# A two-block model on one core: the first expert head's scores from unnormed x, and two loads begun earlier

## The chip, the core and the metric

One core of a Trainium2 chip runs the whole program in one launch. TensorE (PE) multiplies, VectorE (DVE), ScalarE (ACT) and GpSimd (POOL) work beside it, SyncE (SP) issues most loads, POOL the indirect ones. The metric is the device time of one execution in microseconds; less is better. Everything is float32, with 256 tokens of width 1024.

## What is computed

Block 1 mixes attention and a short convolution, and adds an expert layer behind a second norm. Block 2 (two layers of gated attention) follows. The change touches the passage from the mix to the experts:

```python
x = x + gate1 * (y_mix @ w_out)
h2 = rms_norm(x, norm2_w) * (1.0 + scale2) + shift2
x = x + gate2 * peer_ffn(h2, ...)

def peer_ffn(h, ...):                 # by blocks of 128 tokens
    q = (hb @ peer_wq).reshape(B, Q_BLOCK, PEER_HEADS, 2, PEER_HALF)
    s = einsum('bqhpd,hpnd->bqhpn', q, peer_subkeys)   # 8 heads, 2 halves, 128 keys
    vals, idx = lax.top_k(s, 16)
    combo = vals[..., 0, :, None] + vals[..., 1, None, :]
    ...
    top_s, pos = lax.top_k(combo, 16)                  # 16 of 16384 experts a head
    g = softmax(top_s)
    a = gelu(einsum('bqhkd,bqd->bqhk', peer_u[expert], hb))
    return einsum('bqhk,bqhkd->bqd', g * a, peer_v[expert])
```

`mod = silu(c) @ w_ada + b_ada` gives shift, scale and gate (48 column tiles of 128).

## The kernel before

The program is written by hand, engine by engine; the order of the work is the order of the code in five functions (SP, POOL, ACT, PE, DVE), and semaphores tie them. The 256 tokens are two tiles of 128. Up to the experts, x lies turned: `xT[:, c, :]` is chunk c of 8 (128 features) by 256 tokens. `aux` and `pj` are PSUM.

*Output products.* PE computes the eight chunks of `y_mix @ w_out` (`held_out`, `whole`, L1410 to L1412); DVE adds each chunk to `xT` (L2146, the last one in two halves, L2155), with weight splits (L696) and dot products for `mod` (`ada_dots`, L1919) in between; ACT squares it (L1161 to L1167). `out_sums` (PE, L1643) adds the squares by a matrix of ones.

*Second norm.* ACT takes the root (L1170), for both tiles; `second_norm` (DVE) inverts it (L1949) and scales all 16 pieces (L1951, `hT = xT * gain * rstd`); ACT adds the shift (`shift`, L1177). `keep_busy` (L1459) gives PE four products without use meanwhile.

*First head of tile 0.* `early_scores_of_head_0`: 16 query products on PE (L1720) as the chunks get ready, copies on ACT (L1198), two products with the keys (L1726), a copy of the scores (L1200) into `s_all`. `route_in_two` (DVE) finds the 8 best picks first (L2278 to L2263), which lets POOL begin, then the other 8 (L2287 on). `last_ada_tiles` (L1930) computes the last two tiles of `mod` there, which only the end of the expert layer needs.

*The gather.* For each of 2 tiles x 8 heads (16 groups `g`) x 16 picks POOL issues one indirect load (L985): 128 rows of 8 KB, one for each token, the expert's u and v side by side. They lie in 11 or 12 places (`PLACES`, `ROUNDS`: 11 in the first round) cut from memory that the first part leaves; the first 11 wait for what lies there still (for instance `queries` 2 to 8), later ones for `pair_used` of the pick before in that place. For each pick DVE multiplies u by h2 (L2223), ACT sums the row (L1224); four at a time ACT applies gelu (L1235, with a table load) and scales diagonal matrices (L1240), and PE adds v times that diagonal (`sum_pair`, L1694), which frees the place. DVE routes two groups ahead, in quarters between the row products (L2172 to L2209).

*The other scores.* On PE stand, in order: `turn_h2(0)` (L1656), `score_query(0)` for tile 1 (L1669), `score_keys(0)` (L1682), the same for heads 1 and 2 for both tiles, then the sums of picks 0 to 3, with the queries of later heads in between. ACT copies queries (L1186) and scores (L1192) out of PSUM.

*Loads.* SP issues in the order of `LOAD_ORDER`, behind it `last_ada` (two tiles of 512 KB), and four expert weights (`HELD_QUERY` and `LAST_QUERY`, 1 MB each, `SUB_UNITS`), each to places of their own, and the first weight of block 2 (L856 to L863). Behind the gather SP loads block 2's weights.

Of the kernel before, what the change touches and what calls it, by code (L numbers as in the profile page):

```python
# [126 lines left out]
OWN_GROUPS = ((OWN_UNIT, ), (HELD_QUERY, *SUB_UNITS), FIRST_HEADS, (LAST_QUERY, N1))  # L127
EARLY_UNIT = UNITS_1.index(queries_of(2))
# [229 lines left out]
def build(nc, a, out):  # L358
    ctx = ExitStack()
    with ctx:  # L360
# [42 lines left out]
        ystat = sb("ystat", [P, NT, 2])  # L403
        top8 = sb("top8", [P, NT, 8])
# [68 lines left out]
        assert w3.at <= 4096  # L473
        count16 = sb("count16", [P, PICKS], I32)
# [95 lines left out]
        def at(l, per, k):  # L570
# [7 lines left out]
        early_added, early_query, early_query_out, early_scores, early_scores_out = (  # L578
            sem("early_added"), sem("early_query"), sem("early_query_out"), sem("early_scores"), sem("early_scores_out"))
# [235 lines left out]
        def _(sp):  # L815
# [21 lines left out]
            for n in LOAD_ORDER:  # L837
# [168 lines left out]
        def _(act):  # L1006
# [157 lines left out]
            act.wait_ge(early_added, 1)  # L1164
            nc.scalar.activation(sq[:, KC - 1, 0:P], xT[:, KC - 1, 0:P], ACT.Square).then_inc(squares, 1)
            act.wait_ge(taken_dve, KC)
            nc.scalar.activation(sq[:, KC - 1, P:T], xT[:, KC - 1, P:T], ACT.Square).then_inc(squares, 1)  # L1167
            for t, ts in enumerate(halves_):
                act.wait_ge(sums, 2 + t)
                nc.scalar.activation(rstd[:, ts], aux[:, 2 + t, 0:P], ACT.Sqrt, bias=eps[:, 0:1], scale=1.0 / D).then_inc(std_ready, 1)  # L1170
# [223 lines left out]
        def _(pe):  # L1394
# [60 lines left out]
            def keep_busy(n, b):  # L1455

                pe.wait_ge(const_ready, 13)
                for _ in range(n):
# [1170 lines left out]
```

## Time and profile before

| | |
|---|---|
| median of 3 runs | 1158.73 us (1158.66 to 1159.65) |
| span of the profiled execution | 1157.0 us |
| PE, DVE, ACT, POOL busy | 1039.9, 852.6, 704.8, 345.4 us |
| gather: bytes, share of 16 DMA engines | 268.45 MB, 56.0% |
| chain that ended last | PE 53%, DMA 29%, ACT 9%, DVE 7% |

The profile covers one execution; its time is the span beside the runs' median, and its own time outside the span isn't given. The page cuts the span in 40 slices with the busy share of each engine, the granted clock of PE and the bytes that DMA moved. A timeline lists instructions in order of time, merged where they follow each other, with the idle time ahead of them in brackets; the chain of waits follows the last instruction back to what released each step; windows give busy times in a stretch that one chooses. PE entries come in pairs, two for each float32 product.

### The profile page before, as it was taken

The page shows a single profiled execution, that of the slowest core. Times are in us where ns is not written, and L with a number is a line of the kernel's source. Part 1 is how long each engine was busy: PE and PEld are TensorE (multiplying, and loading weights), DVE is VectorE, ACT ScalarE, POOL GpSimd, SP SyncE. Part 2 cuts the span into 40 slices and gives each one's busy share as a digit, 9 for nine tenths or more (in the row PEclk, how much of TensorE's full clock was granted, in tenths as well). Part 3 has the DMA queues.
Part 4 walks back from the last instruction along what each step waited for, and adds up shares of the span by engine and source line. Part 5 has one row for each costly group of instructions (what it writes and reads, how often), then busy time and mean ns, then how long its engine had stood idle before and what let it go on. Part 6 is the DMA issues. An engine that isn't in the chain of part 4 may idle for free.

```text
span 1157.0 us, 13373 instructions
## 1 busy us (share of the span) xinstructions
PE 1039.9 (90%) x4675; PEld 721.1 (62%) x4675; DVE 852.6 (74%) x1535; ACT 704.8 (61%) x1393; POOL 345.4 (30%) x367
## 2 busy tenths in 40 slices
PE   8999999998999869788877878689999999999997
PEld 6999987454455423333333333289788888888885
DVE  7998988776667666666677676646687768886776
ACT  3635835867766766666677666662458555577451
POOL 1001005554554544545544545555000000400000
PEclk9999999999999998889998989999999999999999
DMA  9986879999999999999999999999854654455540
GB/s 372 407 330 241 348 272 395 422 421 421 422 421 421 421 421 422 419 421 412 421 422 421 421 408 423 421 421 421 360 213 167 246 182 182 169 195 184 208 154 37
DMA packets 59557, 390.00 MB, mean 337 GB/s; under 512 B 6882, under 2 KB 7906, under 8 KB 15715
## 3 DMA queue, kind: packets, MB, share of 16 engines
q0 software_dynamic: 36864, 268.45, 56.0%
q1 hardware_dynamic: 21152, 120.10, 27.3%
q8 instruction: 37, 0.61, 0.2%
q10 hardware_dynamic: 1474, 0.60, 0.2%
q14 instruction: 30, 0.24, 0.1%
HBM read 388.08 MB, written 1.05 MB: 336 GB/s over the span
## 4 chain that ended last, share of the span: by engine, by line
PE 53%; DMA 29%; ACT 9%; DVE 7%; issue 2%; SPq 0%; POOL 0%; ACTq 0%; DVEq 0%; POOLq 0%
DMA rows<-in_peer_uv,work 16%; PE aux L1694 14%; DMA low_pairs<-in_peer_uv,work 10%; PE pj L1751 6%; PE pj L1753 6%; PE pj L1752 6%; PE pj L1809 5%; PE aux L1700 3%; PE pj L1810 3%; PE pj L1410 2%; PE pj L1412 2%; PE pj L1411 2%; ACT rows L1224 2%; PE aux L1669 2%; ACT L1235 2%
## 5 line engine op out<-in xcount | busy, mean ns | idle before, releaser
L1694 PE MATMUL aux<-rows,work 128*128 128x512 f32 x504 | 250.6, 648 | 51.6 <-ACT work L1240 51.6
L1694 PEld LDWEIGHTS aux<-rows,work 128*128 128x128 f32 x504 | 101.7, 206 | 186.8 <-issue 118.0
L985 POOL DMA_INDIRECT rows<-in_peer_uv,work x146 | 140.8, 964 | 243.2 <-PE aux L1694 160.1
L1694 PE MATMUL aux<-low_pairs,work 128*128 128x512 f32 x356 | 168.1, 619 | 33.8 <-ACT work L1240 33.8
L1224 ACT ACTIVATE rows<-rows 128x1024 f32<-128x1024 f32 x134 | 141.1, 1053 | 92.0 <-DVE rows L2223 91.8
L1694 PEld LDWEIGHTS aux<-low_pairs,work 128*128 128x128 f32 x356 | 69.2, 198 | 126.9 <-issue 80.4
L765 DVE TENSOR_TENSOR wlo<-wring,whi 128x1024 fp32r<-128x1024 f32 x98 | 121.1, 1251 | 32.3 <-ACT whi L759 31.5
L1224 ACT ACTIVATE low_pairs<-low_pairs 128x1024 f32<-128x1024 f32 x97 | 102.0, 1052 | 65.4 <-DVE low_pairs L2223 65.3
L759 ACT CAST whi<-wring 128x1024 fp32r<-128x1024 f32 x98 | 101.4, 1050 | 50.7 <-PE pj L1810 26.1
L985 POOL DMA_INDIRECT low_pairs<-in_peer_uv,work x101 | 97.5, 966 | 110.2 <-PE aux L1694 92.8
L2223 DVE TENSOR_TENSOR rows<-rows,aux 128x1024 f32<-128x1024 f32 x66 | 79.9, 1219 | 52.1 <-DMA rows<-in_peer_uv,work 51.6
L2223 DVE TENSOR_TENSOR rows<-rows,pj 128x1024 f32<-128x1024 f32 x68 | 82.5, 1218 | 47.5 <-DMA rows<-in_peer_uv,work 47.0
L2223 DVE TENSOR_TENSOR low_pairs<-low_pairs,pj 128x1024 f32<-128x1024 f32 x51 | 62.1, 1219 | 41.8 <-DMA low_pairs<-in_peer_uv,work 41.2
L1809 PE MATMUL pj<-x_parts,whi 128*128 128x512 f32 x256 | 90.9, 398 | 0.1
L1240 ACT ACTIVATE work<-work 128x128 f32<-128x128 f32 x248 | 79.4, 390 | 9.4 <-POOL work L955 4.0
L2223 DVE TENSOR_TENSOR low_pairs<-low_pairs,aux 128x1024 f32<-128x1024 f32 x46 | 55.8, 1219 | 37.7 <-DMA low_pairs<-in_peer_uv,work 37.4
L1410 PE MATMUL pj<-x_parts,whi 128*128 128x256 f32 x256 | 73.4, 287 | 0.3 <-DVE wlo L696 0.2
L1751 PE MATMUL pj<-whi,x_parts 128*128 128x512 f32 x184 | 72.5, 394 | 0.0
L1411 PE MATMUL pj<-x_parts,whi 128*128 128x256 f32 x256 | 72.4, 283 | 0.0
L1412 PE MATMUL pj<-x_parts,wlo 128*128 128x256 f32 x256 | 72.4, 283 | 0.0
L1810 PE MATMUL pj<-x_parts,wlo 128*128 128x256 f32 x256 | 71.8, 280 | 0.0
L1753 PE MATMUL pj<-wlo,x_parts 128*128 128x512 f32 x184 | 71.7, 390 | 0.0
(339 smaller groups left out, 2051.0 us busy)
## 6 DMA issues: line engine op xcount, KB each, us to landing
wring<-in_w SPq DMA_DIRECT2D x74, 1024.0 KB, 4.8
rows<-in_w_ada SPq DMA_DIRECT2D x46, 512.0 KB, 9.4
rows<-in_w SPq DMA_DIRECT2D x3, 1024.0 KB, 11.5
low_pairs<-in_w SPq DMA_DIRECT2D x3, 1024.0 KB, 10.2
rows<-in_peer_uv,work POOLq DMA_INDIRECT x146
work<-in_late_rows SPq DMA_DIRECT2D x2, 1024.0 KB, 9.1
xT<-in_gate_rows SPq DMA_DIRECT2D x2, 1024.0 KB, 8.0
rows<-in_norm_rows SPq DMA_DIRECT2D x2, 1024.0 KB, 6.9
```

What stands on the lines that cost most here:

```text
L759: nc.scalar.copy(layer_part("hi", l, p), layer_raw(l, p)).then_inc(w_hi, 1)
L765: dve.tensor_tensor(layer_part("lo", l, p), layer_raw(l, p), full(layer_part("hi", l, p)), ALU.subtract).then_inc(w_lo["d"], 1)
L985: pool.indirect_dma_start(out=pair(n), out_offset=None, in_=a["peer_uv"], in_offset=bass.IndirectOffsetOnAxis(ap=expert[g % EXPERTS][:, j: ...
L1224: nc.scalar.activation(pair(n)[:, 0:D], pair(n)[:, 0:D], ACT.Copy, accum_out=dots[g % 2][:, j:j + 1]).then_inc(dotted, 1)
L1410: mm(o, w[0], x[0], start=start, stop=False, skip_group_check=skip)
L1411: mm(o, w[0], x[1], start=False, stop=False, skip_group_check=skip)
L1694: ins = mm(peer_sum[t][:, half(c)], diag[:, n % PICKS, :], pair(n)[:, D + c * 512:D + (c + 1) * 512], start=(n % (EXPERT_HEADS * PICKS) == ...
L1751: mm(bank(u), hi[:, k, ts], w_hi_[:, j, :], start=(k == 0), stop=False)
L1753: ins = mm(bank(u), hi[:, k, ts], w_lo_[:, j, :], start=False, stop=(k == last))
L1809: mm(both, w_hi_[:, k, :], x_parts[:, :, k, :], start=(k == 0), stop=False, skip_group_check=True)
L1810: ins = mm(bank(u)[:, 0:T], w_lo_[:, k, :], xh[:, k, :], start=False, stop=(k == KC - 1), skip_group_check=True)
L2223: v.tensor_tensor(row, row, h2_tok[g // EXPERT_HEADS], ALU.mult).then_inc(multiplied, 1)
```

## The change

The scores are linear in h2. For one token, with r its inverse root mean square, h2 = r * (x * gain) + shift2, so the first head's scores are r times those of `x * gain` plus those of the shift. The change computes them so for tile 0:

- ACT writes `xg = xT * gain` behind each square (`gain_x`), and the shift beside it as a 129th column.
- PE runs the 16 query products on `xg` (129 columns) between the sums of squares (`early_products`), in two portions.
- The keys are multiplied with the 128 columns (bank 0) and, spread over all tokens, with the 129th (bank 1); ACT copies the latter to `s_all`, DVE adds the former times r by token (`scores_of_head_0`). r by token is the diagonal of `rstd` (`rstd_by_token`).
- The norm of tile 0 is cut in two halves around `route_first`, tile 1 and `route_rest` follow; ACT's `root(1)` and all shifts stand behind the score copy.
- `keep_busy` goes. `turn_h2(0)` waits for all of the shift of tile 0.
- The last two tiles of `mod` are computed among the output chunks, and `last_ada` and `HELD_QUERY` are loaded behind the queries of head 4, as soon as the mixed input is split.

```diff
+                if n == MIXED_DONE:
+                    sp.wait_ge(mix_split, HC + NT)
+                    sp.dma_start(last_ada, a["w_ada"][RING_TILES:].rearrange("n p d -> p n d")).then_inc(last_ada_loaded, 16)
+                    load_unit(HELD_QUERY)
             sp.wait_ge(proj, M1)
-            sp.dma_start(last_ada, a["w_ada"][RING_TILES:].rearrange("n p d -> p n d")).then_inc(last_ada_loaded, 16)
-            load_unit(HELD_QUERY)
             load_unit(LAST_QUERY)
...
+            def gain_x(c):
+
+                nc.scalar.activation(xg[:, c, 0:P], xT[:, c, 0:P], ACT.Copy, scale=gain[:, c:c + 1]).then_inc(xg_ready, 1)
...
+                if c == 0:
+                    nc.scalar.copy(xg[:, :, P:P + 1], mod[:, 3 * KC:4 * KC].unsqueeze(2)).then_inc(xg_ready, 1)
+                if c < KC - 2:
+                    gain_x(c)
...
-            shift(0)
+            root(0)
             for s in range(2):
                 act.wait_ge(early_query, s + 1)
-                nc.scalar.copy(pq[:, 0, s, 0:P], aux[:, 4 + s, 0:P]).then_inc(early_query_out, 1)
+                nc.scalar.copy(pq[:, 0, s, 0:P + 1], aux[:, 4 + s, 0:P + 1]).then_inc(early_query_out, 1)
             act.wait_ge(early_scores, 1)
-            nc.scalar.copy(s_all[:, 0, :], aux[:, 0, 0:2 * KEYS]).then_inc(early_scores_out, 1)
+            nc.scalar.copy(s_all[:, 0, :], aux[:, 1, 0:2 * KEYS]).then_inc(early_query_out, 1)
+            root(1)
+            shift(0)
             shift(1)
...
             out_sums(4, 5)
-            out_sums(6, 7)
...
+            def early_products(s, chunks):
+
+                for k in chunks:
+                    pe.wait_ge(xg_ready, k + 2)
+                    ins = mm(aux[:, 4 + s, 0:P + 1], query_of_head_0[:, k, s * P:(s + 1) * P], xg[:, k, :], start=(k == 0), stop=(k == KC - 1))
+                return ins
+
+            for s in range(2):
+                early_products(s, range(HC))
+            out_sums(6, 7, tiles=(0, ))
+            for s in range(2):
+                early_products(s, range(HC, KC)).then_inc(early_query, 1)
+            out_sums(6, 7, tiles=(1, ))
...
+                    of_shift = mm(aux[:, 1, s * KEYS:(s + 1) * KEYS], pq[:, 0, s, P:P + 1].broadcast_to([P, P]), k, start=True, stop=True)
+                    ins = mm(aux[:, 0, s * KEYS:(s + 1) * KEYS], pq[:, 0, s, 0:P], k, start=True, stop=True)
...
-            keep_busy(4, 1)
             early_scores_of_head_0()
-            pe.wait_ge(taken_dve, KC)
+            pe.wait_ge(taken_dve, KC + 1)
+            pe.wait_ge(h_ready, 2 * KC)
             turn_h2(0)
...
+            last_ada_tile(1)
+            last_ada_bias()
+            dve.wait_ge(taken_dve, KC + 1)
+            rstd_by_token()
+            second_rstd(0)
+            second_norm(0, range(HC))
+            scores_of_head_0()
...
-            route_in_two()
-            last_ada_tiles()
+            route_first()
+            second_norm(0, range(HC, KC))
+            second_rstd(1)
+            second_norm(1, range(KC))
+            route_rest()
             invert_gate(0)
```

The order of instructions at two places, by the program's own listing (counts are of products here; a line number is that of the kernel named). PE from the last sums of squares to the queries of tile 1, before:

```order
L1643 MATMUL aux<-low_pairs,ones 128x128 x8
L1459 MATMUL aux<-wsT,ident 128x256 x4
L1720 MATMUL aux<-hT,rows 128x128 x16
L1726 MATMUL aux<-rows,pq 128x128 x2
L1656 MATMUL pj<-ident,hT 128x128 x8
L1669 MATMUL aux<-hT,rows 128x128 x16
L1682 MATMUL aux<-rows,pq 128x128 x2
```

and with the change:

```order
L1658 MATMUL aux<-low_pairs,ones 128x128 x4
L1673 MATMUL aux<-work,rows 128x129 x8
L1658 MATMUL aux<-low_pairs,ones 128x128 x2
L1673 MATMUL aux<-work,rows 128x129 x8
L1658 MATMUL aux<-low_pairs,ones 128x128 x2
L1749 MATMUL aux<-rows,pq 128x128
L1750 MATMUL aux<-rows,pq 128x128
L1749 MATMUL aux<-rows,pq 128x128
L1750 MATMUL aux<-rows,pq 128x128
L1686 MATMUL pj<-ident,hT 128x128 x8
L1699 MATMUL aux<-hT,rows 128x128 x16
L1712 MATMUL aux<-rows,pq 128x128 x2
```

The query products have moved ahead of the last sums, the filler (L1459) is gone, and between the key products and the turns stands nothing.

DVE from the last chunk of x to the first routing, before:

```order
L2146 SCALAR_TENSOR_TENSOR xT<-pj,mod,xT 128x256
L2155 SCALAR_TENSOR_TENSOR xT<-pj,mod,xT 128x128 x2
L1949 RECIPROCAL rstd<-rstd 128x128
L1951 SCALAR_TENSOR_TENSOR hT<-xT,gain,rstd 128x128 x8
L1949 RECIPROCAL rstd<-rstd 128x128
L1951 SCALAR_TENSOR_TENSOR hT<-xT,gain,rstd 128x128 x8
L2278 MAX work<-work 128x8 x2
```

and with the change:

```order
L2189 SCALAR_TENSOR_TENSOR xT<-pj,mod,xT 128x256
L2200 SCALAR_TENSOR_TENSOR xT<-pj,mod,xT 128x128 x2
L1955 ISA work,mod<-work,rows 128x1024
L1955 ISA mod 128x1
L1961 TENSOR_TENSOR mod<-mod,cols 128x8
L1986 ISA work,rtok<-rstd,ident 128x128
L1986 ISA rtok 128x1
L1987 RECIPROCAL rtok<-rtok 128x1
L1975 RECIPROCAL rstd<-rstd 128x128
L1981 SCALAR_TENSOR_TENSOR hT<-xT,gain,rstd 128x128 x4
L1994 SCALAR_TENSOR_TENSOR work<-aux,rtok,work 128x256
```

Then DVE behind the first eight picks (L2263 before, L2312 with the change), before:

```order
L2261 TENSOR_TENSOR work<-work 128x128
L2262 TENSOR_REDUCE work<-work 128x2x8
L2263 SCALAR_TENSOR_TENSOR work<-work 128x8
L2287 MATCH_REPLACE work<-work 128x128 x2
L2290 MAX work<-work 128x8 x2
L2293 MAX_INDEX work<-work 128x8 x2
```

and with the change:

```order
L2310 TENSOR_TENSOR work<-work 128x128
L2311 TENSOR_REDUCE work<-work 128x2x8
L2312 SCALAR_TENSOR_TENSOR work<-work 128x8
L1981 SCALAR_TENSOR_TENSOR hT<-xT,gain,rstd 128x128 x4
L1975 RECIPROCAL rstd<-rstd 128x128
L1981 SCALAR_TENSOR_TENSOR hT<-xT,gain,rstd 128x128 x8
L2340 MATCH_REPLACE work<-work 128x128 x2
L2343 MAX work<-work 128x8 x2
```

The norm has gone from ahead of the routing to both sides of it, three quarters of it behind, and the second half of the routing comes after the norm.

## Rows read from the trace of the kernel before

**Rows 1.** Page, part 2, 40 slices of 28.9 us: what DMA moved.

```profile
GB/s 372 407 330 241 348 272 395 422 421 421 422 421 421 421 421 422 419 421 412 421 422 421 421 408 423 421 421 421 360 213 167 246 182 182 169 195 184 208 154 37
```

**Rows 2.** Windows: us, busy us (instructions) of PE, PEld, DVE, ACT, POOL, PEclk, DMA share, GB/s.

```profile
140.00:158.00 18.00, 18.00 (x154) 18.00 (x153) 16.16 (x29) 6.36 (x10) 0.00 (x0) 1.00 0.67 243
160.00:172.50 12.50, 9.94 (x72) 8.98 (x73) 9.66 (x40) 6.57 (x23) 0.16 (x1) 1.00 0.98 394
172.50:174.00 1.50, 1.50 (x16) 1.50 (x15) 1.47 (x10) 0.27 (x1) 1.20 (x2) 1.00 0.11 34
174.00:195.61 21.61, 19.75 (x99) 16.10 (x99) 17.96 (x54) 13.21 (x26) 11.46 (x13) 1.00 0.99 396
195.61:208.20 12.59, 10.58 (x34) 5.99 (x33) 12.38 (x34) 9.15 (x19) 4.88 (x5) 1.00 1.01 419
208.20:218.52 10.32, 10.32 (x34) 6.08 (x33) 8.55 (x13) 6.79 (x16) 4.90 (x5) 1.00 1.01 422
```

**Rows 3.** Chain of waits, 160 to 173 us: start, us, engine, tile, line.

```profile
161.37 0.96 DVE rstd L1949
...
167.87 0.50 PE aux L1726 x2
...
168.39 0.38 ACT work L1200
...
168.80 0.48 DVE work L2278 x2
...
172.34 1.18 POOL rows L985
```

**Rows 4.** Timeline of SP's queue: start, us, line, operation, out<-in, count.

```profile
140.59 1.47 SPq L823 DMA_DIRECT2D rows<-in_w_ada  x2
...
147.89 0.33 SPq L823 DMA_DIRECT2D rows<-in_w_ada  x1
```

**Rows 5.** Timeline of DVE, in brackets the idle time before a row.

```profile
138.72 0.69 DVE L2117 TENSOR_TENSOR x_parts<-work,x_parts 128x512 fp32r<-128x512 f32 x1 [0.44 <-ACT x_parts L1143]
...
155.81 1.22 DVE L1919 CUSTOM_DVE_ANT_0 rows<-rows 128x1024 f32<-128x1024 f32 x1
...
158.91 0.48 DVE L2146 SCALAR_TENSOR_TENSOR xT<-pj,mod,xT 128x256 f32<-128x256 f32 x1 [1.87 <-PE pj L1412]
...
165.44 2.19 DVE L1951 SCALAR_TENSOR_TENSOR hT<-xT,gain,rstd 128x128 f32<-128x128 f32 x8
...
195.62 0.48 DVE L2172 MAX8 work<-work 128x8 f32<-128x128 f32 x2
...
198.08 2.35 DVE L2223 TENSOR_TENSOR low_pairs<-low_pairs,pj 128x1024 f32<-128x1024 f32 x2
```

**Rows 6.** Timeline of PE (two entries for each f32 product).

```profile
158.71 2.35 PE L1643 MATMUL aux<-low_pairs,ones 128*128 128x128 f32 x16
...
168.19 1.04 PE L1656 MATMUL pj<-ident,hT 128*128 128x128 f32 x8
...
171.16 3.84 PE L1669 MATMUL aux<-hT,rows 128*128 128x128 f32 x32 [1.93 <-ACT hT L1177]
```

**Rows 7.** Timeline of ACT.

```profile
168.66 2.44 ACT L1177 ACTIVATE hT<-hT,mod 128x128 f32<-128x128 f32 x8
...
193.65 0.59 ACT L1192 COPY work<-aux 128x512 f32<-128x512 f32 x1 [1.26 <-PE aux L1682]
```

**Rows 8.** Windows around an idle stretch of PE, columns as in rows 2.

```profile
268.50:272.00 3.50, 0.00 (x0) 0.00 (x0) 3.46 (x18) 2.91 (x5) 1.99 (x2) 1.00 1.01 419
272.20:275.60 3.40, 3.40 (x4) 1.38 (x5) 1.99 (x3) 2.88 (x7) 0.00 (x0) 0.52 1.00 417
```

**Rows 9.** Timeline of POOL: issues of gather transfers 11, 15 and 19.

```profile
195.61 0.94 POOL L985 DMA_INDIRECT rows<-in_peer_uv,work  x1 [2.60 <-PE aux L1694]
...
208.20 0.95 POOL L985 DMA_INDIRECT low_pairs<-in_peer_uv,work  x1 [6.50 <-PE aux L1694]
...
218.52 0.95 POOL L985 DMA_INDIRECT rows<-in_peer_uv,work  x1 [4.23 <-PE aux L1694]
```

More of the change, by code:

```diff
@@ L403, in build @@
         ystat = sb("ystat", [P, NT, 2])
+        rtok = sb("rtok", [P, 1])
         top8 = sb("top8", [P, NT, 8])
@@ L473, in build @@
         assert w3.at <= 4096
+        XG_AT = 4096 + EXPERT_HEADS * 2 * KEYS
+        xg = work[:, XG_AT:XG_AT + KC * (P + 1)].rearrange("p (c n) -> p c n", n=P + 1)
         count16 = sb("count16", [P, PICKS], I32)
@@ L1453, in token_major @@
                             ins.then_inc(proj, 1)
-            def keep_busy(n, b):
-                pe.wait_ge(const_ready, 13)
-                for _ in range(n):
-                    mm(aux[:, b, 0:2 * P], ident[:, :], wsT[:, 0:2, :].rearrange("p g t -> p (g t)"), start=True, stop=True)
             pe.wait_ge(const_ready, 3)
@@ L1636, in _, with out_sums @@
                 ins.then_inc(proj, 1)
-            def out_sums(*columns):
+            def out_sums(*columns, tiles=range(NT)):
                 for k in columns:
-                    for t in range(NT):
+                    for t in tiles:
                         pe.wait_ge(squares, k + 1 if k < KC - 1 else KC + t)
@@ L1924, in ada_bias, with last_ada_tile, last_ada_bias @@
                 chain.link(v.tensor_tensor(mod[:, lo:hi], mod[:, lo:hi], cols[:, B_ADA + lo:B_ADA + hi], ALU.add))
-            def last_ada_tiles():
+            def last_ada_tile(c):
                 dve.wait_ge(last_ada_loaded, 16)
-                for c in range(LAST_TILES):
-                    tile = last_ada[:, c, :]
-                    v.tensor_tensor_reduce(tile, tile, cbc, 1.0, 0.0, ALU.mult, ALU.add,
-                                           mod[:, RING_TILES + c:RING_TILES + c + 1]).then_inc(last_ada_used, 1)
+                tile = last_ada[:, c, :]
+                v.tensor_tensor_reduce(tile, tile, cbc, 1.0, 0.0, ALU.mult, ALU.add,
+                                       mod[:, RING_TILES + c:RING_TILES + c + 1]).then_inc(last_ada_used, 1)
+            def last_ada_bias():
                 dve.wait_ge(ada_used, RING_TILES)
@@ L1942, in second_gain, with second_rstd, second_norm, rstd_by_token @@
                 chain.link(v.tensor_tensor(gain[:, :], gain[:, :], cols[:, N2W:N2W + KC], ALU.mult))
-            def second_norm():
-                for t in range(NT):
-                    ts = slice(t * P, (t + 1) * P)
-                    dve.wait_ge(std_ready, 2 + t)
-                    chain.link(v.reciprocal(rstd[:, ts], rstd[:, ts]))
-                    for c in range(KC):
-                        v.scalar_tensor_tensor(hT[:, c, ts], xT[:, c, ts], gain[:, c:c + 1], rstd[:, ts], ALU.mult, ALU.mult).then_inc(h_scaled, 1)
+            def second_rstd(t):
+                ts = slice(t * P, (t + 1) * P)
+                dve.wait_ge(std_ready, 2 + t)
+                chain.link(v.reciprocal(rstd[:, ts], rstd[:, ts]))
+            def second_norm(t, chunks):
+                ts = slice(t * P, (t + 1) * P)
+                for c in chunks:
+                    v.scalar_tensor_tensor(hT[:, c, ts], xT[:, c, ts], gain[:, c:c + 1], rstd[:, ts], ALU.mult, ALU.mult).then_inc(h_scaled, 1)
+            def rstd_by_token():
+                dve.wait_ge(std_ready, 2)
+                chain.link(v.tensor_tensor_reduce(s_left[:, 0, :], rstd[:, 0:P], ident[:, :], 1.0, 0.0, ALU.mult, ALU.add, rtok[:, :]))
+                chain.mark(v.reciprocal(rtok[:, :], rtok[:, :]))
+            def scores_of_head_0():
+                dve.wait_ge(early_query_out, 3)
+                dve.wait_ge(early_scores, 2)
+                chain.wait()
+                v.scalar_tensor_tensor(s_all[:, 0, :], aux[:, 0, 0:2 * KEYS], rtok[:, :], s_all[:, 0, :], ALU.mult, ALU.add).then_inc(early_scores_out, 1)
             for z, x_in in zip((slice(0, HC), slice(HC, KC)), x_loaded):
@@ L2151, in _ @@
                         ada_dots(34 + 2 * c, 36 + 2 * c)
+                    if c == 5:
+                        last_ada_tile(0)
                 else:
@@ L2270, in combine, with route_first @@
                 return z
-            def route_in_two():
-                first, rest = slice(0, FIRST_ROUTED), slice(FIRST_ROUTED, PICKS)
-                lists = [s_all[:, 0, s * KEYS:(s + 1) * KEYS] for s in range(2)]
+            first, rest = slice(0, FIRST_ROUTED), slice(FIRST_ROUTED, PICKS)
+            lists = [s_all[:, 0, s * KEYS:(s + 1) * KEYS] for s in range(2)]
+            def route_first():
                 dve.wait_ge(early_scores_out, 1)
```

39 lines of the change are left out of this document (18 added, 21 removed).

## The prediction

> **What bounds the kernel now.** I read the slices of the page first: the last line of its second part shows some 421 GB/s from about 175 to 810 us [rows 1]. That stretch is the gather of expert rows: 256 transfers of 128 rows by 8 KB, 1.05 MB each, issued by POOL. The windows say the same where it begins: a DMA share of 0.99 to 1.01 and up to 422 GB/s from 174 us on [rows 2]. So the gather is bound by its bytes, 1.05 MB / 421 GB/s = 2.49 us a transfer, and the rest of the program starts when it ends. What this change can win or lose is therefore a shift of that stream: when it starts, and whether its queue runs dry.
>
> Then I read the chain of waits ahead of the stream [rows 3]: the last output chunk on DVE (158.91), sums, root, reciprocal (161.37), norm and shift, the query and key products of the first head on PE, the copy of its scores on ACT (168.39), routing on DVE (168.80), the first gather at 172.34. The windows show what DMA does meanwhile [rows 2]: 394 GB/s from 160 to 172.5 us (the loads begun at 158.9), 34 GB/s until 174.0, then the gather. From 140 to 158 us it moves only 243 GB/s.
>
> **The moved loads.** Two loads of 1.05 MB each go from 158.9 us to behind the fifth head's queries, about 142 us. SP gets there at 142.06 (140.59 + 1.47 [rows 4]), and the wait put ahead of them, for the mixed input's split, ends with DVE's row at 138.72 + 0.69 [rows 5]: SP stalls for nothing, and the loads queued behind lose no time of issue. The room there is 18 us x (421 - 243) GB/s = 3.2 MB, so 2.1 MB fit. What lies behind them in the queue can land later: the last bias tile, issued at 147.89 [rows 4], has 1.6 MB of its own and its predecessor's to wait for (3.7 us) and at worst all of the 2.1 MB (5.0), 156.6, where DVE reads it at 155.81 [rows 5]; at best it is there by 153. I take 0, and keep the worst as a rival. Behind 158.9 remain 2.9 MB, 6.9 us instead of 11.8: DMA is free by about 168. Without this part the earlier gather would still have queued until 172.5. Price 0, cover: that room.
>
> **The first gather.** On PE a product of 128 columns in f32 is two entries of 0.12 us (3.84 us for 32 [rows 6]); 129 columns I take as the same, at most twice that. From the end of the output products at 158.71 [rows 6] PE now has: sums of chunks 4 and 5, 8 entries, 0.97; eight new products 1.94; sums of the last two chunks for tile 0, 0.48 (162.1, root and reciprocals leave the path); eight new products 1.94; sums of tile 1, 0.48 (164.5); then shift and key products, the third of which ACT can take 0.5 after its start, as it took the last key product (167.87 to 168.39 [rows 3]): 165.5. ACT copies 0.41 (168.39 to 168.80 before [rows 3]), DVE's new multiply-add of 256 columns from PSUM is about 0.49, as the one at 158.91 [rows 5]. Routing begins at 166.45 instead of 168.80, and the first gather at **170.0 instead of 172.34, 2.3 us earlier**.
> Beside that path: eight scalings on ACT at about 0.3 each and one tiny copy, where ACT is busy 6.4 of 18 us [rows 2]: 0. The two dot products of the last loaded tiles (1.2 each, as the one at 155.81 [rows 5]) leave DVE's way behind routing; one goes in ahead of chunk 6, into DVE's idle 1.87 us [rows 5], one behind chunk 7 while PE multiplies: 0 to 0.2. The token-wise root (a 128-column reduction and a reciprocal) and the first four norms lie before the scores arrive: 0.
>
> **What is late next.** On DVE the other four norms of tile 0 and all of tile 1 now stand behind the routing, and on ACT all shifts behind the score copy. DVE is free of the routing at 169.75; four norms 1.1 (2.19 for eight [rows 5]), reciprocal 0.96 [rows 3], then eight norms with ACT's shifts behind them, 0.4 + 2.44 [rows 7]: tile 1 is ready at 174.7. PE's next work waits for just that: the queries of tile 1 began at 171.16 [rows 6]. **They begin 3.6 us later**, and behind them stand in order 16 products (3.84), the queries of heads 1 and 2, their keys, and the first sums that free gather places.
>
> And PE has stood idle: its filler of four products is gone, so from 165.6 until the turns at 171.3 nothing runs, 5.7 us. The windows show what 3.5 us of that does [rows 8]: after an empty 268.5 to 272.0 the granted clock is 0.52, the 1.2 GHz level, for 272.2 to 275.6. The turns (1.04 us [rows 6]) run in the same shade and take some of it away. I take 1.0 us on the 3.84 of the first head's queries; bounds 0 (clock back in time) and 1.9 (all of it at the low level).
>
> Now the price of lateness. A gather place is free when PE has summed the row that lay in it, so POOL's issue of transfers 11, 15 and 19 (counted from 0) at 195.61, 208.20 and 218.52 [rows 9] follows PE and not DMA. How full the queue is then comes from the windows [rows 2]:
> - at 195.61: 21.61 us x 396 GB/s = 8.56 MB = 8.16 of 11 transfers: 2.84 left, 7.1 us;
> - at 208.20: 5.28 MB more, 13.19 of 15: 1.81 left, 4.5 us;
> - at 218.52: 4.36 MB more, 17.35 of 19: 1.65 left, 4.1 us.
>
> A transfer needs some reserve before it, or DMA idles. From the start of the stream: 1.7 us from issue (172.34) to the first bytes (174.0), and in the 21.61 us behind it 1.3 us lost (8.56 MB would take 20.3). So the reserve needed lies between 1.7 and 3.0 us; I take the middle, 2.35. The spare is then 4.7, 2.15 and 1.75 us.
> How late are these three issues? Transfer 11 waits for the first sum on PE: 3.6 + 1.0. Transfers 15 and 19 wait for the sums of rows 4 to 8, and these for the second group of row products on DVE (198.08 [rows 5]). In front of that group DVE routes head 2, which began at 195.62 [rows 5] when DVE was free. It needs ACT's copy of head 2's scores (193.65 [rows 7], 0.59 long), which is 3.6 later at 197.25 and done at 197.85: routing 2.25 late, plus the 1.0 of the clock, **3.25 us late**.
> The stream can be ahead of its old place by at most the least of: 2.3 (start), 4.7 - 4.6 = +0.1, 2.15 - 3.25 = -1.1, 1.75 - 3.25 = **-1.5**. The lead is used up at transfer 11 and turns into 1.5 us behind at transfer 19. Later the reserve grows again and the row products wait for DMA themselves, so the compute side's lateness goes, the stream's shift stays. All behind the gather moves with it.
>
> Sum: span 1157.0 + 1.5 = 1158.5 us. The profiled span lies 1.7 under the median of the runs, 1158.73, which I take as constant around it: **1160.2 us**. A measurement tells about 0.2%, 2.3 us; so I forecast no change that it can tell, on the slow side.
>
> **Rivals.**
> 1. *The lead is kept.* The reserve suffices: at the low need of 1.7, without a clock fall, the least is 2.4 - 2.25 = +0.2, and if head 2's score copy were not late as well, the full 2.3 remains. For: DMA shows 419 and 422 GB/s around the two thinnest points, no loss at 4.1 us [rows 2]; the two dot products gone from DVE (2.4 us) quicken it. Against: the order of DVE and ACT, which leaves tile 1 until last. Time: 1158.7 - 2.3 = 1156.4, with half the lead 1157.6.
> 2. *The clock of PE decides* (the slower side). At the low level through all of the first head's queries, 1.9 us, the second group is 4.2 late; at a need of 3.0 the least is 4.1 - 3.0 - 4.2 = -3.0: 1161.8. It decides once the loss passes about 1 us. For: the idle stretch is longer than the one that cost PE its clock [rows 8]; before, PE was idle 1.93 us at most there [rows 6]. Against: the turns may bring the clock back. The Trainium skill (TensorE: Matmul & The Clock Gate, Why this matters for your kernels) advises against idle gaps between bursts of products, since the clock falls back to half; by that rule the taking out of the filler is a fault of the change, and the row at 272.2 agrees. It would put the sum here, by that rule alone, at this rival's 1161.8 rather than the 1159.2 without any fall.
> 3. *The moved loads come late.* At the worst worked out above the last bias tile holds chunk 6 and all behind it by 0.8: 1161.0. For: one queue, one order; against: the 3.2 MB of room.
> 4. *The change does not do what it says*: 129 columns cost double. Then 3.9 us more lie ahead of the routing, the first gather comes at 173.9, later than before, and PE behind it as much: about 1164.
>
> **How the numbers follow.** Forecast 0.51, lead kept 0.17, clock 0.22, loads 0.05, dear columns 0.05. The forecast's own range takes the need from 1.7 to 3.0 and the clock from 0 to 1.9 us: 1158.5 to 1161.8. With part of the lead-kept case (three quarters of the lead) the lower end is 1157.0, and a little past the clock case 1162.4. Faster by over 0.2% (under 1156.4): half of rival 1 and little else, 0.1. Slower (over 1161.05): most of rival 2, rival 4, half of 3 and the forecast's tail, 0.27. Within: 0.63.
>
> **What would show it.** First gather near 170.0; DMA quiet from 168 to 171.7; PE's queries of tile 1 at 174.7 and, if the clock fell, longer than 3.84 with a granted clock under 1; transfer 11 near 200; DMA below 400 GB/s in some stretch between 195 and 222 us. Wrong, if DMA holds 420 there while the first gather is early (then it ends early), or if the first gather itself is not early.

## The result and the profile after

| | before | with the change |
|---|---|---|
| median | 1159.35 us (1158.49 to 1160.16, 21 runs) | 1161.01 us (1159.56 to 1162.67, 21 runs) |
| ratio, 95% interval | | 1.0014 [1.0008, 1.002] |
| span of the profiled execution | 1157.0 us | 1159.2 us |
| first gather issued | 172.34 us | 169.55 us |

The change makes the kernel 1.7 us slower; the forecast was 1160.2 us, 1.5 us over the median it started from. The first gather begins 2.8 us earlier and the stream that follows it still ends later.

The slices of the page look as before [rows 1]; 421 GB/s in most of the gather's slices. The loss is in one place, the seventh and eighth slice (174 to 231 us): 395 and 422 GB/s before, 381 and 372 now.

```profile
GB/s 371 406 333 237 347 295 381 372 423 422 421 422 421 421 422 421 421 422 421 421 419 421 421 413 421 422 420 420 368 207 170 250 181 181 166 198 185 202 158 37
```

The chain of waits up to the first gather, with the change. It answers to [rows 3].

```profile
164.83 0.24 PE aux L1749 x2
...
165.09 0.38 ACT work L1219
...
165.49 0.50 DVE work L1994
...
166.01 0.48 DVE work L2328 x2
```

Routing starts at 166.01 instead of 168.80, 2.8 us earlier. That is the whole gain, and POOL's timeline shows it in the first of these rows (after, transfers 0, 7, 11, 15 and 19; [rows 9] has the last three before):

```profile
169.55 1.28 POOL L991 DMA_INDIRECT rows<-in_peer_uv,work  x1 [53.56 <-DVE work L2312]
...
188.29 1.01 POOL L991 DMA_INDIRECT rows<-in_peer_uv,work  x1 [3.21 <-PE aux L1699]
...
200.23 0.94 POOL L991 DMA_INDIRECT rows<-in_peer_uv,work  x1 [2.00 <-PE aux L1724]
...
211.48 0.94 POOL L991 DMA_INDIRECT low_pairs<-in_peer_uv,work  x1 [5.16 <-PE aux L1724]
...
221.80 0.94 POOL L991 DMA_INDIRECT rows<-in_peer_uv,work  x1 [4.23 <-PE aux L1724]
```

The last three came at 195.61, 208.20 and 218.52 before: they are 4.6, 3.3 and 3.3 us late, and transfer 7, which waits for a query product (L1699), 4.8 us. Its row before:

```profile
183.47 1.01 POOL L985 DMA_INDIRECT rows<-in_peer_uv,work  x1 [0.21 <-PE aux L1669]
```

What DMA does then stands in the windows of after (columns as in [rows 2]):

```profile
169.55:171.00 1.45, 0.03 (x1) 0.06 (x1) 1.45 (x4) 1.28 (x4) 1.28 (x1) 0.50 0.00 0
...
174.00:188.29 14.29, 13.47 (x68) 12.14 (x68) 9.26 (x25) 4.29 (x11) 4.91 (x7) 0.85 1.00 419
188.29:200.23 11.94, 11.16 (x54) 8.86 (x55) 8.99 (x42) 9.16 (x19) 4.26 (x4) 1.00 0.93 338
200.23:211.48 11.25, 10.59 (x34) 6.00 (x33) 11.04 (x24) 9.08 (x19) 4.87 (x5) 1.00 0.99 400
211.48:221.80 10.32, 10.32 (x34) 6.09 (x33) 9.43 (x14) 6.78 (x16) 4.90 (x5) 1.00 0.92 340
...
221.80:229.80 8.00, 8.00 (x26) 4.13 (x25) 3.25 (x3) 6.23 (x15) 6.76 (x8) 1.00 0.98 356
```

Against 421 GB/s the stretch from 188 to 200 us loses 11.94 x (1 - 338/421) = 2.4 us, the next 0.6, then 2.0 and 1.2: 6.1 us in all. So 2.8 us ahead becomes some 3 us behind. I counted the gather's own packets as well: against the kernel before, the first transfer is delivered 2.7 us earlier, the 13th 0.1 us earlier, the 21st 3.1 us later.

Why the issues are late is on PE. Its timeline after answers to [rows 6], the windows below it to [rows 8]:

```profile
164.89 0.39 PE L1750 MATMUL aux<-rows,pq 128*128 128x128 f32 x2
170.97 1.94 PE L1686 MATMUL pj<-ident,hT 128*128 128x128 f32 x8 [5.70 <-ACT hT L1196]
174.09 5.88 PE L1699 MATMUL aux<-hT,rows 128*128 128x128 f32 x32 [1.18 <-ACT hT L1196]
```

```profile
165.30:168.30 3.00, 0.00 (x0) 0.00 (x0) 2.64 (x15) 1.58 (x6) 0.00 (x0) 0.98 0.88 309
168.30:171.00 2.70, 0.03 (x1) 0.06 (x1) 2.60 (x9) 1.28 (x4) 1.28 (x1) 0.50 0.02 9
...
174.10:178.00 3.90, 3.90 (x18) 3.90 (x19) 3.69 (x18) 0.09 (x1) 2.50 (x3) 0.50 0.99 412
178.00:179.00 1.00, 1.00 (x9) 1.00 (x9) 0.77 (x3) 0.17 (x1) 0.00 (x0) 0.80 1.04 418
179.00:182.00 3.00, 2.55 (x18) 2.28 (x17) 0.00 (x0) 1.11 (x3) 0.94 (x1) 1.00 0.99 418
```

The first of these rows is the last key product, the second the turns (`turn_h2`, eight entries), the third the queries of tile 1. PE is idle 5.7 us, its granted clock falls to 0.50, the 1.2 GHz level, and stays there until 178 us, although PE works without a pause from 174. The queries of tile 1 begin 2.9 us later than before and last 2.04 us longer. ACT and DVE hand it on, in the timelines of after that answer to [rows 7] and [rows 5]:

```profile
198.28 0.58 ACT L1211 COPY work<-aux 128x512 f32<-128x512 f32 x1 [1.26 <-PE aux L1712]
```

```profile
157.19 1.23 DVE L1945 CUSTOM_DVE_ANT_0 rows<-rows 128x1024 f32<-128x1024 f32 x1 [0.56 <-DMA rows<-in_w_ada]
...
183.25 0.16 DVE L2286 RECIPROCAL work<-work 128x1 f32<-128x1 f32 x1 [4.41 <-ACT work L1227]
...
198.89 0.49 DVE L2221 MAX8 work<-work 128x8 f32<-128x128 f32 x2 [0.55 <-ACT work L1211]
...
201.37 2.35 DVE L2272 TENSOR_TENSOR low_pairs<-low_pairs,pj 128x1024 f32<-128x1024 f32 x2
```

The copy of head 2's scores is 4.6 us late and DVE's second group of row products 3.3 us (198.08 before). DVE's first group is late by as much (183.33, 179.98 before): it waits 4.41 us for ACT, which copies the late queries first.

### The profile page after: what moved, and what is told of

Its sections match the earlier page's. It is cut to its first block, busy times and chain, and to the rows that moved or that the text cites. A ratio compares the mean times of both kernels' runs of the same rounds, so it can differ in the third digit from the quotient of the medians.

```text
span 1159.2 us, 13379 instructions
## 1 busy us (share of the span) xinstructions
PE 1041.9 (90%) x4671; PEld 723.6 (62%) x4671; DVE 852.9 (74%) x1539; ACT 706.7 (61%) x1402; POOL 344.0 (30%) x367
## 3 DMA queue, kind: packets, MB, share of 16 engines
HBM read 388.08 MB, written 1.05 MB: 336 GB/s over the span
## 4 chain that ended last, share of the span: by engine, by line
PE 54%; DMA 27%; ACT 9%; DVE 6%; issue 2%; SPq 1%; ACTq 0%; DVEq 0%
DMA rows<-in_peer_uv,work 18%; PE aux L1724 15%; DMA low_pairs<-in_peer_uv,work 6%; PE pj L1777 6%; PE pj L1779 6%; PE pj L1778 5%; PE pj L1835 5%; PE aux L1699 4%; PE pj L1836 3%; DMA rows<-in_w_ada 2%; ACT rows L1245 2%; PE pj L1431 2%; PE pj L1432 2%; PE pj L1433 2%; ACT L1256 2%
## 5 line engine op out<-in xcount | busy, mean ns | idle before, releaser
L1724 PE MATMUL aux<-rows,work 128*128 128x512 f32 x504 | 244.9, 636 | 44.2 <-ACT work L1261 44.2
L1724 PE MATMUL aux<-low_pairs,work 128*128 128x512 f32 x356 | 174.4, 639 | 39.2 <-ACT work L1261 39.2
```

Of the source, the lines that this page charges most:

```text
L1724: ins = mm(peer_sum[t][:, half(c)], diag[:, n % PICKS, :], pair(n)[:, D + c * 512:D + (c + 1) * 512], start=(n % (EXPERT_HEADS * PICKS) == ...
```

## The experiments

Two theories stood first. **T1**: PE, DVE and ACT are late, so the issues of transfers 7 to 19 are, the queue runs dry and the early start is lost. **R1**: the moved loads cost the time, with the last bias tile that lands late (the first DVE row above, 0.56 us). A ratio is to the kernel before, run beside it, with its 95% interval; what is read of the stream comes from one profiled execution of each kernel, which can lie up to 1.6 us off the median (the loads back: 1159.84 against 1161.41). One transfer is 1.05 MB, 2.49 us at 421 GB/s.

### Filler where PE idled

```diff
             early_scores_of_head_0()
+            keep_busy(12, 4)
...
             turn_h2(0)
+            keep_busy(3, 4)
             pe.wait_ge(h_ready, 3 * KC)
```

Expected: 

> Changed kernel plus 12 filler products between the early scores and the turns, and 3 between the turns and the first head's queries of tile 1, in the place where PE idled 5.7 and 1.2 us. T1 (late compute work decides: the queries of tile 1, 2.9 us late at their start and 2.0 us longer at the low clock, hand the lateness to the sums and dot products that free the gather's places): the turns take 1.04 instead of 1.94 us, the queries 3.84 instead of 5.88, the second group of dot products comes about 2 us earlier (199.3 instead of 201.37), transfer 19 is issued near 219.8 instead of 221.80, and the time falls by 2 us, to about 1159.0. Rival R1 (the moved loads and the late bias tile cost the time): 1161.0, unchanged. Rival R2 (the order of the norms alone, the clock a side matter because DVE waits for other things): queries 3.84, but the second dots less than 0.7 us earlier and the time 1160.5 or more.

Measured: 1159.63 us, ratio 1.0002 [0.9993, 1.0011]. Its PE timeline (the passage begins 1.0 us later in this execution; DVE was as late at chunk 5 already, 156.01 instead of 155.02, and then waited 0.78 us for the last bias tile, where it was 0.56):

```profile
171.98 1.06 PE L1686 MATMUL pj<-ident,hT 128*128 128x128 f32 x8 [0.53 <-ACT hT L1196]
...
175.09 3.84 PE L1699 MATMUL aux<-hT,rows 128*128 128x128 f32 x32 [0.75 <-ACT hT L1196]
```

Turns and queries take what they took before. Of the loss of 1.7 us the clock is worth some 1.4 (1.0014 against 1.0002, with intervals that overlap a little), where T1 said 2.0. The second group of row products begins at 200.33, 1.0 us earlier, or 2.0 with the late passage taken off. R1 expected no change, and so is not the whole cause; R2 expected less than 0.7 us there and 1160.5 us or more, and is out.

### The loads back at their old place

```diff
-                if n == MIXED_DONE:
-                    sp.wait_ge(mix_split, HC + NT)
-                    sp.dma_start(last_ada, ...).then_inc(last_ada_loaded, 16)
-                    load_unit(HELD_QUERY)
             sp.wait_ge(proj, M1)
+            sp.dma_start(last_ada, ...).then_inc(last_ada_loaded, 16)
+            load_unit(HELD_QUERY)
...
             route_rest()
+            last_ada_tile(0)
+            last_ada_tile(1)
+            last_ada_bias()
```

Expected: 

> Changed kernel with the two loads back at their old place behind the last output chunk, and the two dot products on their tiles and the bias back behind the routing. T1 (late compute work decides at transfers 7 to 19): the stream's first bytes come later, near 172.5 to 173.5, the stream is not ahead at its start, but the issues of transfers 11 to 19 move less than 0.5 us against the changed kernel and the time stays within 0.7 us of it, about 1161.0. R1 (the moved loads and the tile that lands late cost the time): about 1159.0, 2 us faster. A third possibility, that the early start does carry through: 1.5 to 2 us slower, 1162.5 to 1163.

Measured: 1161.41 us, 1.0022 [1.0013, 1.0031]: no faster, so R1 falls. Here the second part of the change is worth nothing that can be told, since what it brings is lost behind it anyway.

### Tile 1 ahead of the rest of tile 0

With the filler (all 15 products in one place); on DVE and PE (ACT's second root and its shifts follow the same order):

```diff
             route_first()
-            second_norm(0, range(HC, KC))
             second_rstd(1)
             second_norm(1, range(KC))
+            second_norm(0, range(HC, KC))
             route_rest()
...
-            pe.wait_ge(h_ready, 2 * KC)
-            turn_h2(0)
-            pe.wait_ge(h_ready, 3 * KC)
+            pe.wait_ge(h_ready, 2 * KC + HC)
             score_query(0)
+            pe.wait_ge(h_ready, 3 * KC)
+            turn_h2(0)
```

Expected: 

> Changed kernel with filler on PE (15 products) and with tile 1's root, reciprocal, norm and shift ahead of the last four chunks of tile 0; PE does the queries of tile 1 ahead of the turns of tile 0. T1: queries of tile 1 begin at about 172.6 instead of 174.09 and take 3.84, so they end at 176.4 instead of 179.97, 3.5 us earlier; second dots near 198, transfer 19 issued near 218.3 to 219; the stream keeps most of its lead of up to 2.8 us and the time is 1157.5 (1156.6 to 1158.5). R1 (loads): 1161.0. R2 (order alone, the clock a side matter): as the run with filler alone less 1.5 us, about 1159.

Measured: 1158.32 us, 0.9993 [0.9984, 1.0002]: inside the expected range, 0.8 us over its middle. The queries began at 173.07, and issues 15 and 19 come only 0.4 us later than in the kernel before. Yet the windows show the queue thin, from issue 15 to 19 and behind 19:

```profile
208.58:218.90 10.32, 10.32 (x34) 6.09 (x33) 10.00 (x14) 6.79 (x16) 4.89 (x5) 1.00 0.97 380
218.90:226.90 8.00, 8.00 (x26) 4.12 (x25) 3.00 (x4) 6.23 (x15) 6.78 (x8) 1.00 0.94 353
```

The stream was 2.5 us ahead when 13 transfers were delivered and 0.2 when 21 were. T1 holds in kind, but a stream that starts earlier needs its later issues earlier too.

### The kernel before, with PE late

```diff
             turn_h2(0)
+            keep_busy(15, 1)
             pe.wait_ge(h_ready, 3 * KC)
             score_query(0)
```

Expected: 

> Kernel before, with 15 filler products between the turns and the first head's queries of tile 1: these then begin near 176.3 instead of 171.16 and end near 180, as in the changed kernel, while the first gather stays at 172.34 and the loads at their old place. T1: the issues of transfers 11, 15 and 19 come at about 200, 211.5 and 221.8, as in the changed kernel, and the time is the changed kernel's within 0.7 us, 1161 (what the early start brings is lost whole at the thin places). If the lead counts one for one: 2.8 us more than the changed kernel, 1163.8. If DMA's backlog hides the lateness (R1): 1159.3, as the kernel before.

Measured: 1161.11 us, 1.0021 [1.0012, 1.003], the changed kernel's time without any part of the change. Lateness on PE is enough, and when it is there the early start is worth nothing that shows. The two are not late by quite the same: issue 15 comes at 210.76 here and at 211.48 in the changed kernel, so up to 0.7 us of a gain could hide in the comparison.

### The moved loads alone

The kernel before with the loads at the mixed split and the dot products on their tiles beside chunks 6 and 7, as in the change.

Expected: 

> Kernel before with the moved loads alone: the two loads issued at the mixed split, one dot product ahead of chunk 6's end and one behind chunk 7, the bias behind them; scores of the first head as before. T1 (how late the compute work frees the places decides, and in the kernel before the row products of group 0 wait for the third and fourth gathered row, 1.2 us each): first gather 172.3 to 172.5, first bytes up to 0.5 us earlier, the 2.6 us freed on DVE at 177.2 end in the waits for those rows; issue of transfer 19 within 0.5 us of the kernel before, time within 0.6 us of it, 1159.0. R1 (moved loads and the bias tile that lands late cost time): 1160.5 to 1161. If the freed DVE time counts: 1157 to 1158.

Measured: 1159.67 us, 1.0007 [0.9998, 1.0016], no difference that can be told. The first gather stays at 172.37, DVE's freed time ends in waits for rows, and issue 19 is where it was. One thing was not expected: PE idles 1.93 us ahead of the queries, as before [rows 6], and here the clock falls.

```profile
171.19 5.47 PE L1672 MATMUL aux<-hT,rows 128*128 128x128 f32 x32 [1.93 <-ACT hT L1180]
```

```profile
172.50:175.90 3.40, 3.40 (x18) 3.40 (x17) 3.23 (x17) 0.27 (x1) 2.79 (x3) 0.50 0.46 123
```

### Tile 1's reciprocal ahead of the scores

The run with tile 1 first, changed further (the rest of tile 0's norm, its turns and ACT's shifts behind tile 1's, as there):

```diff
-            second_norm(0, range(HC))
+            second_norm(0, range(2))
+            second_rstd(1)
             scores_of_head_0()
...
-            keep_busy(15, 4)
+            keep_busy(4, 4)
+            pe.wait_ge(h_ready, KC + 2)
+            turn_h2(0, range(2))
+            keep_busy(9, 4)
```

Expected: 

> The run with tile 1 first, and in it tile 1's reciprocal ahead of the scores' multiply-add (two norms of tile 0 ahead of the scores instead of four) and two of tile 0's eight turns in PE's gap. T1: scores 0.3 us later, queries of tile 1 begin at 172.0 instead of 173.07, copy of head 2's scores near 194.1 instead of 195.37, second dots near 197.1, now set by the landing of the fourth gathered row; transfer 19 issued 0.8 to 1.3 us earlier than in the kernel before (217.2 to 217.7); time 1157.3 (1156.8 to 1158.0). If the reserve of the queue and not the issue decides: no better than the run it is made from, 1158.3.

Measured: 1157.05 us, 0.9986 [0.9977, 0.9995], faster than both kernels. The first gather is at 170.25, 2.1 us ahead of the kernel before; issues 15 and 19 come 0.1 us earlier than there, not 0.8 to 1.3: T1's time came out, its way there did not. The stream is 1.7 us ahead after 21 transfers and 2.1 at its end, with nearly full rate in the same two windows:

```profile
208.10:218.42 10.32, 10.32 (x34) 6.08 (x33) 9.54 (x14) 6.79 (x16) 4.90 (x6) 1.00 1.01 421
218.42:226.42 8.00, 8.00 (x26) 4.12 (x25) 4.20 (x4) 6.23 (x15) 6.79 (x8) 1.00 1.01 415
```

### The same with a late first gather

```diff
                     pool.wait_ge(first_routed, 1)
+                    pool.wait_ge(h_ready, 2 * KC + 2)
```

Expected: 

> The kernel of the previous run with one wait more: POOL issues the first gather only when the first two chunks of tile 0 and all of tile 1 are shifted, near 172, as late as in the kernel before. Tells what the early start itself carries once PE and DVE are early. T1 (the start counts through the landing of the fourth row, that is, for its 1 to 1.3 us and no more): transfer 19 issued as in the kernel before within 0.4 us, time 1158.3 to 1159.0. If the start does not count at all: as the previous run, 1157.3. If it counts in full: 2.3 to 2.8 us more than the previous run, 1159.6 to 1160.

Measured: 1160.39 us, 1.0012 [1.0003, 1.0021]. The wait held the first gather until 173.68, 1.3 us later than in the kernel before and 3.4 later than in the run above:

```profile
173.68 1.18 POOL L992 DMA_INDIRECT rows<-in_peer_uv,work  x1 [57.37 <-ACT hT L1197]
```

The time is 3.3 us more than that run's. So the start counts in full here, and T1's 1 to 1.3 us for it, by way of the fourth row, was wrong. The rival named in the expectation (in full) holds: its 2.3 to 2.8 us were meant for a start near 172.

### Four products of filler

```diff
             early_scores_of_head_0()
+            keep_busy(4, 4)
```

Expected: 

> Changed kernel with four filler products of 256 columns, as many as the change took out, behind the early scores: PE idles 3.8 instead of 5.7 us ahead of the turns. If the taking out of the filler alone cost the clock, it is at 1.0 here (turns 1.04, queries 3.84 us); if the longer wait for the norms does, it falls again (turns up to 1.94, queries over 4.5 us). The 3.5 us gap at 268.5 in the kernel before was followed by the low level, so the second is the likelier; time 1160 to 1161.

Measured: 1162.32 us, in a single run, over the 1160 to 1161 expected. PE idles 3.98 us, and the turns and queries:

```profile
171.11 1.71 PE L1686 MATMUL pj<-ident,hT 128*128 128x128 f32 x8 [3.98 <-ACT hT L1196]
174.23 5.72 PE L1699 MATMUL aux<-hT,rows 128*128 128x128 f32 x32 [1.41 <-ACT hT L1196]
```

In this execution the four products that the change took out do not hold the clock; the longer wait for the norms makes the gap.

### The queries chunk by chunk, from either order

What the runs so far say together is **T2**: the stream keeps its early start whole unless an issue finds the queue nearly empty. Both kernels of this test let PE begin with the first shifted chunk (in the second, 2 stands for `HC`; the filler is 12 products in the first, 4 and 7 in the second):

```diff
                     for k in range(KC):
+                        if h == 0 and s == 0:
+                            pe.wait_ge(h_ready, KC + HC + k + 1)
                         ins = mm(aux[:, 4 + s, ts], ...)
```

The first is made from the run with tile 1 first (start 2.8 us early, lead lost). Expected: 

> The run with tile 1 first (first gather 2.8 us early, which lost its lead at transfers 14 to 20), and in it PE begins the first head's queries of tile 1 with the first shifted chunk instead of the last; 12 filler products instead of 15. The runs so far give a sharper theory, T2: the stream keeps its early start whole as long as each issue from 7 to 19 finds at least about 1.2 transfers in the queue (1.27 found: no loss; 0.8 found: 2.4 us lost), and a lead can be lost but lateness saved beyond that brings nothing. T2 here: queries end near 175.2 instead of 176.9, second dots near 197, issues 15 and 19 about 1 to 1.4 us earlier than in the run it is made from, 1.2 or more transfers left there, the stream 2.5 us or more ahead to its end, time 1156.2 (1155.7 to 1156.9). If the issues alone decide, one for one: 1157.0 to 1157.3. If what was lost in the earlier run was the price of DMA's own sharing with the loads: 1158.3, as that run.

Measured: 1156.92 us, 0.9979 [0.9969, 0.9988]. The queries start at 171.05 instead of 173.07, issue 15 comes 1.2 us earlier than in the kernel before (1.6 earlier than in the parent), and of 2.8 us 2.4 are kept, where the parent kept 0.2. The time lies between the two expectations; the stream speaks for T2, since the issues one for one would leave it 0.2 + 1.6 = 1.8 us ahead. But issue 15 found 1.0 transfers, not the 1.2 expected. The windows of the two stretches:

```profile
206.99:217.31 10.32, 10.32 (x34) 6.08 (x33) 9.75 (x14) 6.78 (x16) 4.91 (x6) 1.00 1.01 414
217.31:225.31 8.00, 8.00 (x26) 4.12 (x25) 4.25 (x6) 6.23 (x15) 6.78 (x8) 1.00 1.01 396
```

The second is made from the run with the reciprocal early (lead kept). Expected: 

> The run with tile 1's reciprocal early (first gather 2.1 us early, no lead lost, 1157.05), with the same start of the queries chunk by chunk; filler 4 and 7 products. T2: issues 15 and 19 come 1 to 1.5 us earlier than in the run it is made from and nothing follows from it, since no issue there found the queue too thin: stream 1.7 to 2.1 us ahead, time within 0.5 us of that run, 1157.0. If the issues decide one for one: 1155.6 to 1156.0.

Measured: 1156.86 us, 0.9983 [0.9974, 0.9992]: issues 15 and 19 come 1.8 us earlier than in its parent and the time is the parent's within 0.2 us, where the issues one for one would have brought about 1 us or more. DMA was at full rate from issue 15 to 19 in both:

```profile
206.31:216.63 10.32, 10.32 (x34) 6.08 (x33) 9.10 (x13) 6.79 (x16) 4.89 (x5) 1.00 1.01 421
```

An issue ahead of need is worth nothing, as T2 said.

### The loads back once more, where the lead is kept

The second of these two, with the edit of the second experiment. Expected: 

> The run with tile 1's reciprocal early and the queries chunk by chunk (1156.86), with the two moved loads back at their old place and the dot products on their tiles back behind the routing: the second part of the change undone where the first one keeps its lead. T2 (the early start counts in full unless an issue finds less than about 1.1 transfers queued): the stream's first transfers 0.4 to 1.0 us later, since the loads still move when the gather starts; the 2.6 us more on DVE end for the most part in the wait for the fourth gathered row, second dots 0 to 1 us later, 1.2 to 1.6 transfers left at issue 15, so no further loss: 0.4 to 1.2 us more than the run it is made from, 1157.3 to 1158.0. If the loads' place is worth nothing: 1156.9. If DVE's 2.6 us come in whole, the queue runs thin again: 1158.5 or more.

Measured: 1158.06 us, 0.9992 [0.9983, 1.0001], 1.2 us more (1.0 by the ratios, whose intervals overlap). The first gather is issued at the same time (170.04), but the stream is 1.3 instead of 2.3 us ahead, from its first transfers on, with 418 GB/s or more from issue 11 to 8 us behind issue 19. So the moved loads are worth about 1 us, once nothing takes it away; the stream shows it more clearly than the times do.

### The runs side by side

Times against the kernel before, us (first gather, issue 15, and the time at which the gather's packets have delivered 21 transfers; minus is earlier). "Left" is worked out as in the prediction, the issue's number less GB/s x us of the windows since the gather's first bytes, in transfers.

| run | first gather | issue 15 | left at 15 | GB/s 15 to 19 | left at 19 | GB/s in 8 us behind 19 | stream at 21 |
|---|---|---|---|---|---|---|---|
| before | 0 | 0 | 1.81 | 422 | 1.65 | 421 | 0 |
| the change | -2.8 | +3.3 | 0.42 | 340 | 1.08 | 356 | +3.1 |
| filler | -1.8 | +2.3 | 0.71 | 365 | 1.11 | 366 | +2.0 |
| four products of filler | -2.7 | +3.3 | 0.46 | 356 | 0.95 | 347 | +3.0 |
| loads back | -2.7 | +3.4 | 0.32 | 356 | 0.82 | 372 | +2.4 |
| tile 1 first | -2.8 | +0.4 | 0.62 | 380 | 0.88 | 353 | -0.2 |
| before, PE late | 0 | +2.6 | 0.58 | 371 | 0.92 | 348 | +2.1 |
| loads alone | 0 | 0 | 1.58 | 421 | 1.43 | 423 | -0.6 |
| reciprocal early | -2.1 | -0.1 | 1.12 | 421 | 0.98 | 415 | -1.7 |
| late first gather | +1.3 | +3.4 | 1.08 | 415 | 0.99 | 377 | +2.5 |
| chunks, tile 1 first | -2.8 | -1.2 | 1.01 | 414 | 0.93 | 396 | -2.4 |
| chunks, reciprocal early | -2.3 | -1.9 | 1.62 | 421 | 1.48 | 422 | -2.3 |
| the same, loads back | -2.3 | -0.8 | 1.48 | 422 | 1.32 | 418 | -1.3 |

With 1.3 transfers or more left the rate is whole (418 GB/s or more), with under 0.8 left at issue 15 it falls to between 340 and 380; around 1.0 both occur. The thin place of the changed kernel begins before this table does: counted the same way it had 0.56 transfers left at issue 7 and 0.71 at issue 11, where the kernel before had 3.77 and 2.84.

## Why the prediction was right, and where it was not

- *What bounds the kernel.* Right: in all twelve profiled executions the span moves, against the kernel before, as the gather's last packet does, within 0.6 us, from 2.8 us shorter (last packet 3.4 earlier) to 3.4 longer (3.2 later). The shift at transfer 21 is a rougher guide: the filler run is 2.0 us behind there, 0.9 at its end, and its median is 0.2 us slower by the ratio.
- *Moved loads, price 0.* Right for this kernel: the run without them and the run with them alone differ from their parents by nothing that can be told. DMA stands still at 169.55 to 171, as forecast. The mechanism of rival 3 came true (0.56 us of wait, chunk 6 at 159.49 instead of 158.91), without its price: DVE reads tile 0's root at 162.72, and at 162.77 in the run with chunks and the reciprocal early, where nothing waited for the tile.
- *First gather.* Forecast 170.0, measured 169.55. 16 entries of 129 columns took 1.95 us (filler run), half of the 3.84 for 32 of 128: rival 4 is out.
- *What is late next.* Right: the queries of tile 1 at 174.09 (174.7), issue 11 at 200.23 (near 200), the second row products 3.29 us late (3.25). That the last two hit so closely is luck: the queries begin 2.9 us late, not 3.6, and the clock takes 2.0 us, not 1.0.
- *Clock.* Right in kind, the term mis-sized: 1.0 us taken with bounds of 0 and 1.9, measured 2.04 on the queries. The upper bound was no bound: queries that ran whole at half the clock would take twice 3.84 us, as the turns nearly did (1.94 for 1.04), so "all of it at the low level" costs 3.8; only the clock's return at 178 us kept it at 2.04. What the forecast set against the fall, the turns that "may bring the clock back", did not: they ran at 0.50 themselves. The Trainium skill (TensorE: Matmul & The Clock Gate, Why this matters for your kernels) warns of such gaps; the trace agrees, and filling the gap gave some 1.4 us back.
- *The price of lateness.* The step that failed in its parts is "the least of" the spares. First, it begins with transfer 11: transfers 7 to 10 wait for query and key products on PE as well, and transfer 7 is 4.8 us late. Its end of the lead at transfer 11 (+0.1) agrees with what was measured at transfer 13, but most of that was lost from 188 to 200 us, behind issue 7, for which the forecast has no term. Second, the reserve: 2.35 us, or 0.94 transfers, the middle of two bounds, lies where the table turns. But the sum takes away only what the reserve is short of, -1.5 us at transfer 19, where 3.1 were measured. In the run with tile 1 first the same sum gives 1.75 - 0.38 = 1.4 us ahead, and 0.2 were left. In the seven runs of the table that fell to between 340 and 380 GB/s behind issue 15 or 19 the stream stood 0.7 to 1.6 us worse at transfer 21 than this sum gives. A larger reserve of 3.5 us would give these seven within 0.5 us, but would leave "reciprocal early" and "chunks, tile 1 first" only 0.7 and 1.8 us ahead, where 1.7 and 2.4 were measured. So it stays open whether a thin place costs extra or the reserve is larger than forecast and has no sharp edge.
- *The sum.* 1.5 us forecast, 1.7 measured as a median and 2.2 in the profiled span. That it came so near is partly luck: the sum was 1.6 us short at transfer 21, and the profiled stream gave back as much, 3.1 us behind there, 2.1 at transfer 161 and 1.7 at its end. I did not follow that up; the kernel before loses about 0.7 us between transfers 100 and 160 of its profiled execution against several of the runs.
- *Rivals.* "The lead is kept" names what the later runs do: with PE's work early enough 1157 us comes out, near its 1156.4 to 1157.6. "The clock decides" was more of the truth than its chance of 0.22: its own condition, a loss past about 1 us, was met with 2.04, filling the gap took some 1.4 of the 1.7 us away, and 1161.0 lies halfway between its 1161.8 and the forecast's 1160.2. But it was not alone: the run with PE late by filler, at full clock throughout (queries 3.73 us), was as slow.

## What to carry to other kernels

An earlier start of a stream that is bound by its bytes is worth what the thinnest point of its queue leaves of it: before moving the start, list every later issue that waits for compute, from the first, and keep about one and a half transfers queued at each (in this kernel 1.3 or more kept the full rate). Work put off to make the start early belongs in the order in which the waiters of those issues need it; here the other tile's norm ahead of the rest of this tile's, products that begin with the first chunk, and filler in PE's gap together turned 1.7 us slower into 2.0 to 2.4 us faster. And where a wait grows on PE, fill it whole (15 products held the clock here, four did not), or count the queue of products behind it at the lower clock.

## What was not expected of the hardware

- The granted clock stayed at 0.50 for 7 us after PE had work again (171 to 178 us, with one gap of 1.2 us in it), and with four products of filler the window from 171.2 to 178.2 shows 0.51. A gap of 1.93 us was followed by full clock in one execution and by 0.50 in another of nearly the same code; gaps of up to 1.36 us, met at full clock, were not followed by a fall.
- DMA does not slow down in proportion to what is missing: around one transfer (1.05 MB, 2.49 us) left in the queue its rate is 414 to 421 GB/s in some stretches and 347 to 396 in others. Which of its parts idles then was not looked at.
